# Deeper attention order, forget row as one fp32r product, squares taken from the accumulators, row norms with the factor last, and late weight splits moved, in a two-block fp32 kernel

## Chip, core and metric

The kernel runs on one core of a Trainium2 chip. The metric is the device time of one execution in microseconds. TensorE does the matmuls, VectorE (DVE), ScalarE (ACT) and GpSimd (POOL) the rest, SyncE (SP) issues most DMAs. The engines run side by side and meet at semaphores.

## What is computed

A sequence of 256 tokens of width 1024 passes a first stack of two layers and then one block of a second stack. Everything is fp32. Cut to what matters here:

```python
# layer 1 ("odd"): two kinds of attention side by side, then an output product
q, k, v, fl, cq, ckv, kr = split(x @ odd_w_in)
fcum = cumsum(log_sigmoid(fl + fgate_b))                 # 8 heads with a forget gate
s_fox = q @ k.T * 64 ** -0.5 + fcum[:, None] - fcum[None, :]   # causal, softmax, @ v
q2 = rms_norm(cq, q_norm_w) @ w_uq                       # 8 heads from latents, with rope
k2, v2 = rms_norm(ckv, kv_norm_w) @ w_ukv
x = layer_norm(alpha * x + concat(o_fox, o_mla) @ odd_w_out)
x = layer_norm(alpha * x + swiglu(x))                    # ffn0, ffn1: one per layer
# second stack, one block
h = x + mod2 * rmsnorm(short_gated_conv(modulate(rmsnorm(x, g0), mod0, mod1)), g1)
y = h + mod5 * rmsnorm(squared_relu_mlp(modulate(rmsnorm(h, g2), mod3, mod4)), g3)
```

The term of the query position in `s_fox` is the same for a whole softmax row, so the kernel adds only the key's, `neg_f`, of size 8 x 256 (one row for each head).

## The kernel before

**Weights.** All weights come in chunks (1 MB where nothing else is said), in one list in the order of their use. For each chunk SP loads `raw`, ACT copies it to `hi` in fp32r (L1130), DVE computes `lo` = raw - hi (L1559), and TensorE makes three fp32r products for every tile (hi with hi, hi with lo, lo with hi: L562 to L564 with the weights standing in the array, L569 to L571 with the activations there). There are six slots of such chunks, four in some stages. `split(upto)` in the ACT stream and in the DVE stream says how far the splitting has come; a call does all chunks up to the one named, in that engine's order, and ACT, DVE and TensorE each run their own program in order. So where a `split` stands decides what it delays. A TensorE product of a chunk waits for `lo_split`.

**Attention (profile 383 to 491 us).** `ODD_STEPS` is an order written by hand that all engines walk through: projections (`proj`), the norms of the two latents (`qn_sum`, `qn_out`, `kvn_sum`, `kvn_out`), the products from the latents (`uq`, `mla`), attention steps (`att`) and rows of the output product (`rows`). In step `att a` TensorE computes the scores of head a (L990 to L994), turns the probabilities of head a-1 (L1002) and multiplies those of head a-2 with the values (L1014, L1016). Heads 0 to 7 have the forget gate: each of the two score tiles (128 queries by 128 or 256 keys) is a plain fp32 product of `qz` and `kf` plus a second plain fp32 product that adds row a of `neg_f` to all queries (L991). DVE masks and finds the row maximum (L1964, L1968), ACT takes exponentials (L1417), DVE divides by the sum (L1973, L1975), TensorE turns, ACT copies the turned tile (L1432), TensorE multiplies, ACT and DVE split the outputs of each pair of heads (`o_hi`, `o_low`). `scores(a)` waits for the mask of head a-2. Heads 10, 11 and 12 have no other TensorE work between them.

**Latent norms.** ACT empties a projection bank into `cq` or `ckv` (L1368, L1370); at `qn_sum` and `kvn_sum` it squares those tiles (L1143), TensorE sums the squares with a column of ones (L676), ACT takes the root (L1149, with a change of the activation table before it, L1136), DVE the reciprocal (L1584), TensorE spreads it (L687), and DVE and ACT scale and split the latent (L1590, L1157, L1599).

**Row norms of the second stack.** `pre` and `preff` (the inputs of the convolution and of the MLP), `post` and `postff` (their outputs). Tokens lie in two halves h of 128, columns in two halves n of 512. `rms_std` on ACT squares all 1024 columns of a half with an accumulated sum (L1175) and takes the root (L1177). `modulated` on DVE waits for it, multiplies x with 1/rms and the scale row (L1680), then adds the shift row (L1685); `add_post` does the same from the accumulators (L1695, L1700). `turn` on TensorE (L660) turns the result, ACT and DVE split it (L1163, L1658), and the next products start. `ln_sum` and `ln_rest` are the layer norm ahead of `pre`. In this stretch DVE's `split(first["sc"] + 2)` and `split(first["mlp"] + 2)` stand before `modulated` of half 0.

**Other splits.** In the short convolution's third round (q = 3) `split(c + 3)`, `split(c + 4)` and `split(c + 5)` split the last three output chunks. In the MLP the first output chunk is split in round i = 3, after the turned hidden tiles (`mlp_hi`, `mlp_low`, L1515, L2080); in the last round the third-last output chunk is split after `mlp_hi(15)` and `mlp_low(15)`. Each TensorE round is a projection (`col`) and then rows of the output product.

The end of the chain is `postff`: square, root, reciprocal, two scalings, two additions for half 1, and four stores.

## Time and profile before

| | us |
|---|---|
| median of 3 runs | 1007.55 (1007.19 to 1009.74) |
| the profiled execution | 1008.01 |
| its span, first to last instruction | 1006.2 |
| TensorE busy | 962.0 |
| DVE busy | 644.7 |
| ACT busy | 461.5 |
| POOL busy | 59.4 |
| mean granted TensorE clock | 0.988 |

The span is 1.8 us shorter than the profiled execution's time, and that is 0.5 us above the median. "Busy" counts matmuls that lie in each other's pipeline once. A line of the timeline gives start, length, engine, line of the kernel, operation and tiles, how many records are merged (x16), and in brackets how long the engine was idle before it and what it waited for. Matmuls overlap in the pipeline: what one costs in a row of them is the distance from start to start, not its length. A plain fp32 product has two records. The granted clock is 1.00 at 2.4 GHz and 0.50 at 1.2 GHz.

### The profile page before, as it was taken

Reading aid. Unit: us, or ns where it says so; the run is one execution under the profiler, and the core shown is the slowest. Engines: PE = TensorE matmul, PEld = TensorE weight load, DVE = VectorE, ACT = ScalarE, POOL = GpSimd, SP = SyncE. Lnnn points to the kernel's source line nnn. Section 1 sums busy time; section 2 is a strip of 40 time slices with the busy share of each in tenths; the row PEclk is TensorE's granted clock in tenths of the full one; section 3 lists DMA queues with packets and bytes.
Section 4 is the critical chain, followed back from the end, with each engine's and each line's share of the span. In section 5 each row is a group of like instructions: output and inputs, shape, how many; then the busy total and the mean of one; then the engine's idle time right before and its main releaser. Section 6 shows DMA issues by size and latency. Waiting matters only on the chain.

```text
span 1006.2 us, 15135 instructions
## 1 busy us (share of the span) xinstructions
PE 962.0 (96%) x6561; PEld 876.1 (87%) x6561; DVE 644.7 (64%) x732; ACT 461.5 (46%) x553; POOL 59.4 (6%) x79
## 2 busy tenths in 40 slices
PE   6999989999999999999899999999899999999996
PEld 6999779999999899776699989997899888999884
DVE  5966895545455853565659778688677765455444
ACT  6456744443435355644454343445354434444342
POOL 2033000000000000120030000000000000000000
PEclk9999999999999999899999999999999999999999
DMA  8743466555564643212479999985455454565621
GB/s 259 242 131 126 159 196 218 180 184 193 175 202 128 188 147 111 84 43 85 153 279 329 387 310 343 306 320 194 172 179 179 145 183 163 176 201 170 204 87 42
DMA packets 122282, 190.52 MB, mean 189 GB/s; under 512 B 6566, under 2 KB 103080, under 8 KB 119144
## 3 DMA queue, kind: packets, MB, share of 16 engines
q1 hardware_dynamic: 115184, 156.94, 48.3%
q0 software_dynamic: 5616, 31.78, 8.6%
q8 instruction: 52, 0.85, 0.4%
q10 hardware_dynamic: 1416, 0.83, 0.3%
q14 instruction: 14, 0.11, 0.0%
HBM read 188.49 MB, written 1.05 MB: 188 GB/s over the span
## 4 chain that ended last, share of the span: by engine, by line
PE 79%; DVE 11%; ACT 6%; issue 2%; DMA 1%; DVEq 0%; ACTq 0%; POOL 0%
PE PS L562 15%; PE PS L564 15%; PE PS L563 15%; PE PS L569 9%; PE PS L570 9%; PE PS L571 9%; DVE lo L1559 4%; ACT hi L1130 2%; PE PS L695 1%; PE PS L660 1%; DMA raw<-even_w_in 1%; ACT hid L1417 1%; DVE r L1629 1%; PE PS L1014 1%; DMA sq<-norm_gains 1%
## 5 line engine op out<-in xcount | busy, mean ns | idle before, releaser
L1559 DVE TENSOR_TENSOR lo<-raw,hi 128x2048 fp32r<-128x2048 f32 (+2 forms) x150 | 336.0, 2259 | 163.8 <-ACT hi L1130 163.5
L562 PE MATMUL PS<-x_hi,hi 128*128 128x256 f32 x1320 | 376.1, 285 | 2.1 <-DVE x_lo L1756 2.1
L564 PE MATMUL PS<-x_hi,lo 128*128 128x256 f32 x1320 | 373.9, 283 | 0.0
L563 PE MATMUL PS<-x_lo,hi 128*128 128x256 f32 x1320 | 373.2, 283 | 0.0
L1130 ACT ACTIVATE hi<-raw 128x2048 fp32r<-128x2048 f32 (+2 forms) x150 | 277.8, 1879 | 8.5 <-DMA raw<-even_w_in 6.4
L562 PEld LDWEIGHTS PS<-x_hi,hi 128*128 128x128 f32 x1320 | 251.9, 191 | 4.5 <-DVE lo L1559 2.4
L563 PEld LDWEIGHTS PS<-x_lo,hi 128*128 128x128 f32 x1320 | 252.7, 191 | 1.7 <-issue 0.5
L564 PEld LDWEIGHTS PS<-x_hi,lo 128*128 128x128 f32 x1320 | 251.8, 191 | 0.0
L569 PE MATMUL PS<-hi,hid_hi 128*128 128x512 f32 x352 | 141.5, 402 | 6.0 <-DVE lo L1559 5.5
L570 PE MATMUL PS<-lo,hid_hi 128*128 128x512 f32 x352 | 139.8, 397 | 0.0
L571 PE MATMUL PS<-hi,hid_lo 128*128 128x512 f32 x352 | 139.1, 395 | 0.0
L569 PE MATMUL PS<-hi,x_hi 128*128 128x256 f32 (+1 forms) x256 | 82.8, 324 | 7.5 <-DVE x_lo L1658 3.4
L569 PEld LDWEIGHTS PS<-hi,hid_hi 128*128 128x128 f32 x352 | 66.6, 189 | 23.9 <-issue 9.5
L570 PE MATMUL PS<-lo,x_hi 128*128 128x256 f32 (+1 forms) x256 | 80.7, 315 | 0.0
L571 PE MATMUL PS<-hi,x_lo 128*128 128x256 f32 (+1 forms) x256 | 80.5, 315 | 0.0
L571 PEld LDWEIGHTS PS<-hi,hid_lo 128*128 128x128 f32 x352 | 66.5, 189 | 15.4
L570 PEld LDWEIGHTS PS<-lo,hid_hi 128*128 128x128 f32 x352 | 66.4, 189 | 15.1 <-issue 1.2
L569 PEld LDWEIGHTS PS<-hi,x_hi 128*128 128x128 f32 x256 | 49.8, 194 | 13.4 <-issue 8.1
L1215 ACT ACTIVATE gate_s<-PS 128x512 f32<-128x512 f32 x20 | 12.0, 598 | 104.0 <-PE PS L564 104.0
L571 PEld LDWEIGHTS PS<-hi,x_lo 128*128 128x128 f32 x256 | 49.7, 194 | 2.9
L570 PEld LDWEIGHTS PS<-lo,x_hi 128*128 128x128 f32 x256 | 49.7, 194 | 2.6
L1220 ACT ACTIVATE hid_hi<-hid 128x512 fp32r<-128x512 f32 x20 | 12.6, 632 | 81.6 <-DVE hid L1734 81.6
(276 smaller groups left out, 833.5 us busy)
## 6 DMA issues: line engine op xcount, KB each, us to landing
raw<-ffn_w_gate SPq DMA_DIRECT2D x22, 1024.0 KB, 5.4
raw<-ffn_w_up SPq DMA_DIRECT2D x22, 1024.0 KB, 5.4
raw<-ffn_w_down SPq DMA_DIRECT2D x22, 1024.0 KB, 5.0
raw<-mlp_w_in SPq DMA_DIRECT2D x16, 1024.0 KB, 5.6
raw<-mlp_w_out SPq DMA_DIRECT2D x16, 1024.0 KB, 5.0
sq<-ada_w POOLq DMA_DIRECT2D x12, 1024.0 KB, 6.2
r<-ada_w POOLq DMA_DIRECT2D x12, 1024.0 KB, 6.7
raw<-sc_w_in SPq DMA_DIRECT2D x12, 1024.0 KB, 5.3
```

The lines of the kernel that those rows point to most:

```text
L562: pe.matmul(dst, wh, hi, start=start, stop=False, skip_group_check=True)
L563: pe.matmul(dst, wh, lo, start=False, stop=False, skip_group_check=True)
L564: return pe.matmul(dst, wl, hi, start=False, stop=stop_, skip_group_check=True)
L569: pe.matmul(dst, hi, wh, start=start, stop=False, skip_group_check=True)
L570: pe.matmul(dst, hi, wl, start=False, stop=False, skip_group_check=True)
L571: return pe.matmul(dst, lo, wh, start=False, stop=stop_, skip_group_check=True)
L660: last = pe.transpose(PS[:, 2 * h + n, j * P:(j + 1) * P], src[:, h, o:o + P], ident)
L695: last = pe.matmul(PS[:, bank + n, :], ones[:, :], modrow[:, m, n * HB:(n + 1) * HB], start=True, stop=True)
L1130: act.activation(split_view("hi", c), split_view("raw", c), ACT.Copy).then_inc(hi_split, 1)
L1215: act.activation(gate_s[:, i % 2, :, :], bank2(6 - 2 * (i % 2)), ACT.Silu).then_inc(silu, 1)
L1220: act.activation(hid_hi[:, i % 3, :, :], hid[:, i % 2, :, :], ACT.Copy).then_inc(hi_done, 1)
L1559: dve.tensor_tensor(split_view("lo", c), split_view("raw", c), split_view("hi", c).bitcast(F32), ALU.subtract)\
```

## The change

- **Order of attention.** Step a turns head a-2 and multiplies head a-3; ACT copies the turned tile before the exponentials of head a; DVE masks head a, then divides head a-1. The pair outputs come one step later, and there is one more step, `att 18`.
- **Forget row.** `neg_both` holds the fp32r high part of `neg_f` in rows 0 to 7 and the rest in rows 32 to 39, for 128 and 256 keys side by side (384 columns); `pick` has ones in rows a and 32 + a of column a. One fp32r matmul per head opens both score tiles.
- **Squares of the latents.** ACT squares the projection bank right before it empties it; the kv squares get tiles of their own.
- **Row norms.** ACT squares each 512 columns as they come, turns the first sum into a bias with an Identity, and takes the root of the second plus that bias. DVE multiplies with the row first, and after the reciprocal does factor and add in one instruction per 512 columns. The unused square goes to PSUM (`rms_in`) or to `sq` (`rms_out`).
- **Splits.** `sc + 2` and `mlp + 2` on DVE go behind `turned_lo` of half 0; the convolution's last output chunks are split one place earlier; the MLP's first output chunk before the turned hidden tiles; its third-last one before the last `mlp_hi`/`mlp_low`.

```diff
@@ -98,13 +98,15 @@
         head_vec = sb("head_vec", [16, 4])
+        pick = sb("pick", [P, FOX_H], F32R)
...
         moments = sb("moments", [P, 2, 2])
-        sumsq = sb("sumsq", [P, 2])
+        sumsq = sb("sumsq", [P, 4])
+        part_sq = sb("part_sq", [P, 2])
@@ -156,6 +158,7 @@
             neg_f = sb("neg_f", [P, S], F32, odd)
+            neg_both = sb("neg_both", [P, 384], F32R, odd)
@@ -347,7 +350,7 @@
             ("mla", i) for i in range(5, 11)] + [("att", 8), ("rows", 0), ("att", 9), ("rows", 1), ("att", 10), ("att", 11),
-            ("att", 12), ("rows", 2), ("att", 13), ("att", 14), ("rows", 3), ("att", 15), ("att", 16), ("att", 17)]
+            ("att", 12), ("rows", 2), ("att", 13), ("att", 14), ("rows", 3), ("att", 15), ("att", 16), ("att", 17), ("att", 18)]
@@ -389,7 +392,7 @@
                     "op": ("ln0", "ln1", "ln2", "pre", "preff")}
-        EACH = {"r": 4, "st": 4, "mv": 2, "sq": 2, "std": 2, "t": 4, "x": 4, "turned": 4, "hi": 4, "lo": 4}
+        EACH = {"r": 4, "st": 4, "mv": 2, "sq": 6, "std": 2, "t": 4, "x": 4, "turned": 4, "hi": 4, "lo": 4}
@@ -666,7 +669,8 @@
                 else:
-                    parts = [([sq[:, 2 * q, :], sq[:, 2 * q + 1, :]], "sq", q + 1, 2) for q in range(t // 2)]
+                    o = 4 if name == "kvn" else 0
+                    parts = [([sq[:, o + 2 * q, :], sq[:, o + 2 * q + 1, :]], "sq", q + 1, 2) for q in range(t // 2)]
@@ -975,7 +979,7 @@
                 if a == 0:
-                    pe.wait_ge(sem("neg_f_ready"), 1)
+                    pe.wait_ge(sem("neg_f_ready"), 2)
@@ -983,12 +987,14 @@
                 b = a % 2
+                if a < FOX_H:
+                    pe.matmul(PS[:, b, 0:384], pick[:, a:a + 1].to_broadcast([P, P]), neg_both[:, :], start=True, stop=False,
+                              skip_group_check=True)
...
                     if a < FOX_H:
-                        pe.matmul(dst, qz[:, a, qs], kf[:, a // 2, 0:kw], start=True, stop=False)
-                        last = pe.matmul(dst, ident[:, a:a + 1].to_broadcast([P, P]), neg_f[:, 0:kw], start=False, stop=True)
+                        last = pe.matmul(dst, qz[:, a, qs], kf[:, a // 2, 0:kw], start=False, stop=True, skip_group_check=True)
@@ -1019,10 +1025,10 @@
                     scores(a)
-                if 1 <= a <= 16:
-                    turn_prob(a - 1)
-                if a >= 2:
-                    attend(a - 2)
+                if 2 <= a <= 17:
+                    turn_prob(a - 2)
+                if a >= 3:
+                    attend(a - 3)
@@ -1170,12 +1176,29 @@
-            def rms_std(name, h, src):
-                act.activation(r_tok[:, h, :], src, ACT.Square, accum_out=sumsq[:, h:h + 1]).then_inc(sig(name, "sq"), 1)
-                act.wait_ge(*sig_at(name, "sq", h + 1))
-                act.activation(std[:, h:h + 1], sumsq[:, h:h + 1], ACT.Sqrt, bias=eps_sb[:, 1:2], scale=1.0 / D)\
+            def rms_std(name, h, src, unused, ready):
+                for n in range(2):
+                    ready(n)
+                    act.activation(unused(n), src(n), ACT.Square, accum_out=sumsq[:, 2 * h + n:2 * h + n + 1])\
+                       .then_inc(sig(name, "sq"), 1)
+                    if n == 0:
+                        act.wait_ge(*sig_at(name, "sq", 3 * h + 1))
+                        act.activation(part_sq[:, h:h + 1], sumsq[:, 2 * h:2 * h + 1], ACT.Identity, bias=eps_sb[:, 1:2],
+                                       scale=1.0 / D).then_inc(sig(name, "sq"), 1)
+                act.wait_ge(*sig_at(name, "sq", 3 * h + 3))
+                act.activation(std[:, h:h + 1], sumsq[:, 2 * h + 1:2 * h + 2], ACT.Sqrt, bias=part_sq[:, h:h + 1], scale=1.0 / D)\
                    .then_inc(sig(name, "std"), 1)
+            def rms_in(name, before, h):
+                rms_std(name, h, lambda n: x_tok[:, h, n * HB:(n + 1) * HB], lambda n: PS[:, 2 * h + n, :],
+                        lambda n: act.wait_ge(*sig_at(before, "x", 2 * h + n + 1)))
+            def rms_out(name, which, h):
+                rms_std(name, h, lambda n: PS[:, 2 * h + n, :], lambda n: sq_all[:, n * HB:(n + 1) * HB],
+                        lambda n: wait_acc(act, which, h, n))
@@ -1365,25 +1388,22 @@
                 elif p <= 8:
+                    act.activation(sq[:, 2 * (p - 7):2 * (p - 7) + 2, :], bank, ACT.Square).then_inc(sem("norm_sq"), 1)
...
                 elif p == 9:
+                    act.activation(sq[:, 4:6, :], bank, ACT.Square).then_inc(sem("norm_sq"), 1)
...
             def qn_sum(_):
-                act.wait_ge(sem("odd_evac"), 9)
-                squares(cq, 4)
...
             def kvn_sum(_):
-                act.wait_ge(sem("odd_evac"), 10)
-                act.wait_ge(*norm("qn", "var", 1))
-                squares(ckv, 2)
@@ -1423,15 +1443,15 @@
             def attention(a):
+                if 2 <= a <= 17:
+                    act.wait_ge(sem("prob_turned"), a - 1)
+                    if a >= 4:
+                        act.wait_ge(sem("attended"), a - 3)
+                    act.activation(prob_t[:, a % 2, :], PS[:, 2, 0:384], ACT.Copy).then_inc(sem("prob_t_ready"), 1)
...
                     exps(a)
-                if 1 <= a <= 16:
-                    act.wait_ge(sem("prob_turned"), a)
-                    if a >= 3:
-                        act.wait_ge(sem("attended"), a - 2)
-                    act.activation(prob_t[:, (a - 1) % 2, :], PS[:, 2, 0:384], ACT.Copy).then_inc(sem("prob_t_ready"), 1)
-                if a >= 3 and a % 2:
-                    o_hi((a - 3) // 2)
+                if a >= 4 and a % 2 == 0:
+                    o_hi((a - 4) // 2)
@@ -1449,12 +1469,10 @@
             split(first["sc"] + 2)
-            act.wait_ge(*sig_at("ln3", "x", 2))
-            rms_std("pre", 0, x_tok[:, 0, :])
+            rms_in("pre", "ln3", 0)
...
             ln_std("ln3", 1)
-            act.wait_ge(*sig_at("ln3", "x", 4))
-            rms_std("pre", 1, x_tok[:, 1, :])
+            rms_in("pre", "ln3", 1)
@@ -1476,7 +1494,7 @@
                 c = at["sc", "c", q]
-                split(c + 3)
+                split(c + 3 + (q == 3))
@@ -1486,7 +1504,7 @@
                     sc_hi(0)
-                split(c + 4)
+                split(c + 4 + (q == 3))
@@ -1496,13 +1514,10 @@
             for h in range(2):
-                for n in range(2):
-                    wait_acc(act, "sc", h, n)
-                rms_std("post", h, PS[:, 2 * h:2 * h + 2, :].rearrange("p a n -> p (a n)"))
+                rms_out("post", "sc", h)
...
                     split(first["mlp"] + 2)
-                act.wait_ge(*sig_at("post", "x", 2 * h + 2))
-                rms_std("preff", h, x_tok[:, h, :])
+                rms_in("preff", "post", h)
@@ -1515,6 +1530,7 @@
+            split(c + 4)
@@ -1526,6 +1542,8 @@
                 act.activation(relu_s[:, i % 3, :, :], bank2(4 + i % 3), ACT.Relu).then_inc(sem("mlp_relu"), 1)
+                if i == NM - 1:
+                    split(c + 3)
@@ -1533,9 +1551,7 @@
             for h in range(2):
-                for n in range(2):
-                    wait_acc(act, "mlp", h, n)
-                rms_std("postff", h, PS[:, 2 * h:2 * h + 2, :].rearrange("p a n -> p (a n)"))
+                rms_out("postff", "mlp", h)
@@ -1672,33 +1688,33 @@
-            def modulated(name, h, shift, scale):
+            def modulated(name, before, h, shift, scale):
+                for n in range(2):
+                    dve.wait_ge(*sig_at(before, "x", 2 * h + n + 1))
+                    dve.tensor_tensor(half(r_tok, h, n), half(x_tok, h, n), modrow[:, scale, n * HB:(n + 1) * HB], ALU.mult)\
+                       .then_inc(sig(name, "t"), 1)
...
                 for n in range(2):
-                    dve.scalar_tensor_tensor(out=half(r_tok, h, n), in0=half(x_tok, h, n), scalar=rstd[:, h:h + 1],
-                                             in1=modrow[:, scale, n * HB:(n + 1) * HB], op0=ALU.mult, op1=ALU.mult)\
-                       .then_inc(sig(name, "t"), 1)
-                for n in range(2):
                     dve.wait_ge(*sig_at(name, "t", 2 * h + n + 1))
-                    dve.tensor_tensor(half(r_tok, h, n), half(r_tok, h, n), modrow[:, shift, n * HB:(n + 1) * HB], ALU.add)\
+                    dve.scalar_tensor_tensor(out=half(r_tok, h, n), in0=half(r_tok, h, n), scalar=rstd[:, h:h + 1],
+                                             in1=modrow[:, shift, n * HB:(n + 1) * HB], op0=ALU.mult, op1=ALU.add)\
...
                     wait_acc(dve, which, h, n)
+                    dve.wait_ge(*sig_at(name, "sq", 3 * h + 1 + 2 * n))
+                    dve.tensor_tensor(half(r_tok, h, n), PS[:, 2 * h + n, :], modrow[:, gate, n * HB:(n + 1) * HB], ALU.mult)\
+                       .then_inc(sig(name, "t"), 1)
...
                 for n in range(2):
-                    dve.scalar_tensor_tensor(out=half(r_tok, h, n), in0=PS[:, 2 * h + n, :], scalar=rstd[:, h:h + 1],
-                                             in1=modrow[:, gate, n * HB:(n + 1) * HB], op0=ALU.mult, op1=ALU.mult)\
-                       .then_inc(sig(name, "t"), 1)
-                for n in range(2):
                     dve.wait_ge(*sig_at(name, "t", 2 * h + n + 1))
-                    dve.tensor_tensor(half(x_tok, h, n), half(x_tok, h, n), half(r_tok, h, n), ALU.add)\
-                       .then_inc(sig(name, "x"), 1)
+                    dve.scalar_tensor_tensor(out=half(x_tok, h, n), in0=half(r_tok, h, n), scalar=rstd[:, h:h + 1],
+                                             in1=half(x_tok, h, n), op0=ALU.mult, op1=ALU.add).then_inc(sig(name, "x"), 1)
@@ -1905,7 +1921,8 @@
             base = first["odd"]
-            dve.memset(neg_f[:, :], 0.0)
+            dve.memset(neg_both[:, :].bitcast(F32), 0.0)
+            dve.tensor_tensor(pick[:, :], ident[:, 0:8], ident[:, 32:40], ALU.add)
@@ -1915,8 +1932,11 @@
                     link(dve.tensor_tensor(small[0:8, 3, :], small[0:8, 2, :], small[0:8, 1, :], ALU.add))
-                    dve.tensor_tensor_scan(neg_f[0:8, :], small[0:8, 3, :], small[0:8, 3, :], 0.0, ALU.add, ALU.bypass)\
-                       .then_inc(sem("neg_f_ready"), 1)
+                    link(dve.tensor_tensor_scan(neg_f[0:8, :], small[0:8, 3, :], small[0:8, 3, :], 0.0, ALU.add, ALU.bypass))
+                    for o, n in ((0, P), (P, S)):
+                        link(dve.tensor_copy(neg_both[0:8, o:o + n], neg_f[0:8, 0:n]))
+                        dve.tensor_tensor(neg_both[32:40, o:o + n], neg_f[0:8, 0:n], neg_both[0:8, o:o + n].bitcast(F32),
+                                          ALU.subtract).then_inc(sem("neg_f_ready"), 1)
@@ -1983,9 +2003,10 @@
                     masked(a)
-                    normalised(a)
-                if a >= 3 and a % 2:
-                    o_low((a - 3) // 2)
+                if 1 <= a <= 16:
+                    normalised(a - 1)
+                if a >= 4 and a % 2 == 0:
+                    o_low((a - 4) // 2)
@@ -2000,14 +2021,14 @@
             ln_rest("ln3", 0)
-            split(first["sc"] + 2)
-            modulated("pre", 0, 0, 1)
+            modulated("pre", "ln3", 0, 0, 1)
...
             turned_lo("pre", 0)
+            split(first["sc"] + 2)
...
             dve.memset(cv[:, :, :, 1 + S:2 + S], 0.0).then_inc(sem("cv_pad"), 1)
-            modulated("pre", 1, 0, 1)
+            modulated("pre", "ln3", 1, 0, 1)
@@ -2044,13 +2065,13 @@
                 i, c = q % 2, at["sc", "c", q]
-                split(c + 3)
+                split(c + 3 + (q == 3))
...
                 dve.wait_ge(sem("cv_ready"), q)
-                split(c + 4)
+                split(c + 4 + (q == 3))
@@ -2062,11 +2083,11 @@
             add_post("post", "sc", 0, 2)
+            modulated("preff", "post", 0, 3, 4)
+            turned_lo("preff", 0)
             split(first["mlp"] + 2)
-            modulated("preff", 0, 3, 4)
-            turned_lo("preff", 0)
             add_post("post", "sc", 1, 2)
-            modulated("preff", 1, 3, 4)
+            modulated("preff", "post", 1, 3, 4)
@@ -2080,6 +2101,7 @@
+            split(first["mlp"] + 4)
@@ -2089,6 +2111,8 @@
                    .then_inc(sem("mlp_hid"), 1)
+                if i == NM - 1:
+                    split(c + 3)
```

## Rows read from the trace of the kernel before

**Rows 1.** The page, busy time by engine (share of the span) and instructions.
```profile
PE 962.0 (96%) x6561; PEld 876.1 (87%) x6561; DVE 644.7 (64%) x732; ACT 461.5 (46%) x553; POOL 59.4 (6%) x79
```

**Rows 2.** Windows: length, busy PE, PEld, DVE, ACT, POOL, granted clock, DMA.
```profile
401.10:404.50 3.40, 3.40 (x13) 2.67 (x12) 0.64 (x4) 1.70 (x3) 0.00 (x0) 0.50 0.39 158
...
838.00:841.40 3.40, 3.40 (x10) 2.63 (x9) 1.61 (x2) 0.00 (x0) 0.00 (x0) 0.50 0.52 183
```

**Rows 3.** Timeline of TensorE, scores of head 0.
```profile
383.69 0.39 PE L991 MATMUL PS<-neg_f,const 128*128 128x128 f32 x2
383.91 0.60 PE L990 MATMUL PS<-kf,qz 128*128 128x256 f32 x2
```

**Rows 4.** Timeline of TensorE, head 8 and output rows of 512 columns.
```profile
454.24 0.82 PE L994 MATMUL PS<-km,qm 96*128 96x128 f32 x4
...
456.44 0.40 PE L570 MATMUL PS<-lo,x_hi 128*128 128x512 f32 x1
456.68 0.40 PE L571 MATMUL PS<-hi,x_lo 128*128 128x512 f32 x1
```

**Rows 5.** Timeline at the sums of the latent squares, ACT and TensorE.
```profile
398.60 1.14 ACT L1143 ACTIVATE sq<-cq 128x512 f32<-128x512 f32 x2
399.27 1.95 PE L676 MATMUL PS<-ones,sq 128*128 128x1 f32 x16 [1.20 <-ACT sq L1143]
...
401.54 1.28 ACT L1417 ACT_TABLE_LOAD   x1
...
419.58 1.02 PE L676 MATMUL PS<-ones,sq 128*128 128x1 f32 x8 [2.27 <-ACT sq L1143]
```

**Rows 6.** Waits of TensorE: total us, times, longest.
```profile
PE PS L1002 <- DVE hid L1975: 5.0, 4, 2.2
```

**Rows 7.** Timeline of the late heads and the drain, DVE and TensorE.
```profile
474.11 2.29 DVE L1559 TENSOR_TENSOR lo<-raw,hi 128x2048 fp32r<-128x2048 f32 x1 [1.43 <-ACT hi L1130]
...
479.02 0.55 PE L1002 MATMUL PS<-const,hid 128*128 128x128 f32 x3 [2.24 <-DVE hid L1975]
...
485.40 0.49 PE L1002 MATMUL PS<-const,hid 128*128 128x128 f32 x3
...
491.24 0.50 PE L569 MATMUL PS<-hi,x_hi 128*128 128x512 f32 x1 [0.93 <-DVE x_lo L1980]
```

**Rows 8.** Timeline of TensorE, its waits among the rope steps.
```profile
439.52 0.36 PE L952 MATMUL PS<-hid_hi,hi 128*96 128x256 f32 x1 [0.62 <-DVE kr L1946]
...
442.02 1.10 PE L943 MATMUL PS<-qm,const 96*96 96x256 f32 x4 [0.84 <-DVE qm L1956]
```

**Rows 9.** Timeline of DVE, scaling and splitting q's latent: first and last.
```profile
406.60 0.68 DVE L1590 TENSOR_TENSOR cq<-cq,PS 128x512 f32<-128x512 f32 x1
...
410.66 0.69 DVE L1599 TENSOR_TENSOR hid_lo<-r,hid_hi 128x512 fp32r<-128x512 f32 x1 [0.39 <-ACT hid_hi L1157]
```

**Rows 10.** Timeline before the short convolution, DVE and TensorE.
```profile
701.94 2.28 DVE L1559 TENSOR_TENSOR lo<-raw,hi 128x2048 fp32r<-128x2048 f32 x1
...
706.40 1.26 PE L660 MATMUL PS<-const,r 128*128 128x128 f32 x8 [2.89 <-DVE r L1685]
...
708.89 0.55 PE L569 MATMUL PS<-hi,x_hi 128*128 128x256 f32 x1 [1.23 <-DVE x_lo L1658]
```

**Rows 11.** Timeline of TensorE where it waited for a split of output weights.
```profile
794.97 0.47 PE L569 MATMUL PS<-hi,hid_hi 128*128 128x512 f32 x1 [0.78 <-DVE lo L1559]
...
836.95 0.47 PE L569 MATMUL PS<-hi,hid_hi 128*128 128x512 f32 x1 [2.13 <-DVE lo L1559]
...
985.07 0.47 PE L569 MATMUL PS<-hi,hid_hi 128*128 128x512 f32 x1 [2.21 <-DVE lo L1559]
```

**Rows 12.** Timeline of TensorE, the turn before the MLP.
```profile
806.87 1.26 PE L660 MATMUL PS<-const,r 128*128 128x128 f32 x8 [0.46 <-DVE r L1685]
```

**Rows 13.** Timeline of the closing norm, half 1, ACT and DVE.
```profile
999.32 1.02 ACT L1175 ACTIVATE r<-PS 128x1024 f32<-128x1024 f32 x1 [6.93 <-PE PS L571]
...
1002.42 1.28 DVE L1700 TENSOR_TENSOR x_tok<-x_tok,r 128x512 f32<-128x512 f32 x2
```

## The prediction

> **What bounds the kernel now.** I read the busy shares first, then TensorE's waits, then the granted clock, then the timeline at each gap. TensorE is busy for 96% of the span [rows 1]; DVE and ACT have room almost everywhere. So an edit gains only what it takes from TensorE's own work or from one of its few gaps, and work saved elsewhere is worth nothing. The gaps stand in five places, and the diff touches all of them: the attention stage (383 to 491 us), the norm before the short convolution (703 to 720), the norm between it and the MLP (795 to 820), the MLP's opening and end (837, 985), and the closing norm. Everything between them is an unbroken row of matmuls, which shifts as a block.
>
> A gap costs twice. After several gaps the granted clock is 0.50, that is 1.2 GHz and not 2.4, for a stretch of 3.4 us [rows 2]; five such stretches touch this diff (from 401.1, 421.6, 479.6, 708.3 and 838.0). Where TensorE has work for the whole stretch, it loses half of it, 1.7 us.
>
> **Attention stage: what goes.**
> - *Forget row.* Per head the two fp32 products with the forget row run over 128 and 256 columns. The 128-column one takes 0.22 us (383.69 to 383.91 [rows 3]), so both take 0.66. In their place stands one fp32r matmul of 384 columns. Fp32r matmuls of 512 columns follow each other at 0.24 us (456.44, 456.68 [rows 4]), so 384 take 0.18. That is 0.48 us for each of 8 heads: **3.8 us**, all on TensorE's path. The price is four small DVE instructions (copy, subtract, twice) behind the scan and three at the stage's start, well before the first head; DVE has idle time there.
> - *Squares at the accumulators.* ACT now squares the projection while it empties the bank, so at the sums TensorE no longer waits: 1.20 us at 399.27 and 2.27 us at 419.58 [rows 5], **3.5 us**. ACT's work is the same, only earlier; banks come free some 0.6 us later, but TensorE comes back to a bank after two more projections.
> - *Clock.* The stretches from 401.1 and 421.6 come right behind these two waits. With the waits gone I take both away: **3.4 us**.
> - *Deeper order.* TensorE waits 5.0 us in 4 places for the normalised probabilities [rows 6], and the third half-clock stretch follows the longest of them, 2.24 us at 479.02 [rows 7]: 1.7 us. Both are at stake: **6.7 us**. Two short waits for the rotary part (0.62 at 439.52, 0.84 at 442.02 [rows 8]) hang on DVE finishing the softmax of the same step; it no longer has to, which frees DVE about 1 us earlier: **1.4 us**.
>
> **Attention stage: what comes back.** The sum is 18.8 us, and TensorE, once ahead, meets the chains behind it.
> - Before `uq(0)`: from the first scaling to the last low half of q DVE and ACT need 4.75 us (406.60 to 411.35 [rows 9]), and both arrive late because two table loads (1.28 us each [rows 5]) and the exponentials of head 2 lie ahead. TensorE has only the kr projection and head 3 to cover it: a new wait of 1.4 us.
> - At the kv sum ACT still has the split of `w_ukv`, two evacuations, and a table load before and behind the root. TensorE waits for the reciprocal, for the probabilities of head 3 and, at head 2's output, for the bank that `o_low(0)` reads: some 2.2 us together.
> - Late heads: a split still sits in the DVE stream at head 12 (474.11 [rows 7]); the probabilities after it come 1.7 us too late even for the deeper order. Before head 8's output 0.6 us is added, since its bank waits for `o_low(3)`.
> - The drain: from the last scores (485.40) to the first output row (491.24) one head's whole chain takes 5.84 us [rows 7]. The deeper order leaves one more turn and output in it, which fills idle time, but the output of head 14 now also stands behind the chain of pairs: I take the drain as 6.6 us, and 1.4 us of the removed wait as not gained.
>
> Together 7.3 us come back, 11.5 net; a walk through the stage step by step gives 12.4. I take **12 us**. The ends: 18.8 if all new waits are covered, 6 if DVE and ACT are as late as they are now (then forget row and half the rest remain).
>
> **Norm before the short convolution.** Now: DVE splits a weight chunk (701.94, 2.2 us), then reciprocal, two scalings, two additions; TensorE's turn starts at 706.40 after 2.89 us, its first matmul at 708.89 [rows 10]. After: the product with the scale row needs no root and is done while ACT squares; the split goes behind; behind the root stand a reciprocal and one 0.7 us instruction. The root comes about when it does now (the two half squares need one more read and a small Identity, but the first starts 0.7 us earlier), just before the split ends at 704.2; so the first half comes at 704.5 and not 706.3, and the first matmul at 707.2: 1.7 us earlier. But the split now stands before the second half's `ln_rest`, which takes back 1.3; the second half comes only 0.7 to 0.9 us earlier and TensorE waits there instead. **0.9 us**, and the half clock from 708.3 changes nothing in it, since it only fills that wait.
>
> **Norm before the MLP.** The split of the last convolution weights moves ahead of the last convolution: the wait of 0.78 at 794.97 goes [rows 11]. The chain for half 0 (square, root, factor, add, square, root, factor, add, with a 2.2 us split inside) ends at 806.87 with a wait of 0.46 [rows 12]. With the split behind it and the factor last it is done by 803, while TensorE still has rows of half 1. The turn to first matmul time stays. 0.78 and 0.46 and what the second half gives: **1.4 us**.
>
> **MLP opening and end.** At 836.95 TensorE has waited 2.13 us for the split of the first output chunk, and a half-clock stretch follows from 838.0 [rows 2, 11]. The split now stands before the turned hidden tiles. Its data have been there for 20 us, ACT and DVE are idle in front of it, and `mlp_low(1)`, which it delays by about 1 us, is still done before TensorE is through the projection: 2.1 + 1.7 = **3.8 us**. At 985.07 the wait is 2.21 [rows 11]; the split moves ahead of `mlp_hi(15)` into idle time: **2.2 us**.
>
> **Closing norm.** Now after the last matmul: a square of 1024 (from 999.32), root, reciprocal, two scalings, two additions from 1002.42 to 1003.7 [rows 13]. After: half of the square and one product are done before; behind the last matmul remain a square of 512, the root, a product that now ends at about 1000.8, reciprocal, and two factor-and-add of 0.7: end at 1002.35. **1.4 us**.
>
> **A rule of the notes.** The new code puts an Identity between Square and the root. In this trace the exchange of tables costs 1.28 us each time [rows 5], and no row shows an Identity while the root's table is in. The Trainium skill, "ScalarE: Activation LUTs", in its section on table sets says that cheap functions such as identity are in every set, so no load would come. If it were otherwise, two loads in each of six norms would be a rival, priced below from the row.
>
> **Sum.** 12 + 0.9 + 1.4 + 3.8 + 2.2 + 1.4 = 21.7 us. The new waits (1.4, 2.2 and 1.7 us) are of the kind that brought the half clock before (2.24 us did): I take one new stretch, 1.7 us, so 20.0. The profiled execution took 1008.01 with a span of 1006.2; the median is 1007.55, 0.5 less. 1008.0 - 20.0 - 0.5 = **987.5 us**.
>
> **Rivals.**
> 1. *The clock keeps falling.* Three or more of the new gaps bring a half-clock stretch. For it: gaps of 1.2 to 2.3 us did so. Against: gaps of 2.21 us (985.07) and 0.9 to 1.6 us elsewhere did not. Two more stretches, 3.4 us: 991. The Trainium skill, "TensorE: Matmul & The Clock Gate", lets the clock fall only after a long idle gap; the trace shows it falling after 2.24 us, so the row decides.
> 2. *DVE and ACT bind in attention*, and the stage gives 6 and not 12: 993.5.
> 3. *All new waits are covered*: the stage gives 17 and no stretch is added, 6.7 us more than forecast: 981.
> 4. *Identity forces a reload*: 2 x 1.28 in each of six norms, of which about five are exposed: 12.8 us back, 1000.
> 5. *Slower: the heads become serial.* ACT's exponentials of head a now stand behind the copy of head a-2, and that behind TensorE's turn. If this closed into a ring with no overlap, each of 14 heads would take the 5.84 us of one chain [rows 7]. For heads 8 to 15 that is 47 us plus 8 for two splits, against 37 now (454.24 to 491.24 [rows 4, 7]), +18, with nothing left of the 12: 1008 - 9.7 + 18 = 1016. It decides only from 4.8 us a head on. Against it: the ring spans two steps, the scores of a+1 wait only for the mask of a-1, and the probabilities of a-2, which the turn needs, are finished while head a-1 is scored.
>
> **How the numbers follow.** The forecast (20 us, give or take 3) 0.58, rival 1 0.13, rival 2 0.13, rival 3 0.10, rival 4 0.03, rival 5 0.03. Range 981.5 to 994. A change under 0.3% (3 us) can't be told from none here. Faster by more 0.96, same 0.01, slower 0.03.
>
> **What would show it.** Forget row: one fp32r matmul of 384 columns per head, 0.18 us to the next. Squares: no wait before the sums, no half clock behind them. Order: TensorE's waits for probabilities under 2 us in all, and the first output row 12 us earlier. MLP: no wait at the first output chunk nor at the third-last one, no half clock. Closing norm: 1.3 us less between the last matmul and the end. The prediction is wrong if attention yields under 8 us, if table loads appear in the norms, or if gaps of over 2 us appear where there were none.

## The result and the profile after

Over 6 runs each, the kernel before takes 1007.94 us (1006.21 to 1009.74) and the changed one 980.84 us (979.70 to 983.36): ratio 0.973, interval 0.9711 to 0.975, or 25 to 29 us. The profiled execution of after took 980.15 us. The forecast was 987.5 us with a range from 981.5: the direction was right, the time came out 6.7 us shorter than forecast, and the range ended 0.7 us too high.

The page of after, busy time by engine, as [rows 1]:

```profile
PE 944.3 (97%) x6537; PEld 862.8 (88%) x6537; DVE 645.9 (66%) x737; ACT 466.6 (48%) x577; POOL 62.0 (6%) x79
```

TensorE's waits in after (line, releaser: total us, times, longest), as [rows 6]:

```profile
PE PS L572 <- DVE lo L1575: 3.9, 4, 1.9
PE PS L572 <- DVE x_lo L1674: 3.5, 3, 1.2
PE PS L663 <- DVE r L1701: 2.6, 2, 1.7
PE PS L1008 <- DVE hid L1995: 2.5, 3, 1.1
PE PS L565 <- issue: 1.3, 1, 1.3
```

The 5.0 us for probabilities have become 2.5 us in three places. Waits for latent squares are gone. L572's waits for `lo`, split weights, are what remains of 8.8 us before; their longest is 1.9 where it was 2.2, and the 1.9 stands in work that the change doesn't touch (127 us).

Windows over the stages of after (length, busy PE with its matmuls, granted clock, DMA share, GB/s), and, from before, its attention stage:

```profile
380.00:476.00 96.00, 87.35 (x569) 1.00 0.29 94
476.00:688.00 212.00, 209.68 (x1408) 1.00 0.87 306
688.00:708.00 20.00, 16.86 (x135) 1.00 0.44 143
708.00:787.00 79.00, 79.00 (x566) 1.00 0.57 184
787.00:812.00 25.00, 23.87 (x198) 1.00 0.55 194
```
```profile
383.00:491.00 108.00, 96.44 (x588) 0.95 0.25 84
```

In after the clock stands at its upper level, 2.4 GHz, through all of them; the five stretches that the prediction lists have no successor. One more, in work that the change doesn't touch, is in both profiles (134.8 us in before, 133.5 in after). TensorE's busy time in attention fell by 9.1 us (96.44 to 87.35): 3.8 of it is the forget row (as forecast), 5.1 the three stretches of 3.4 us in which matmuls ran at 1.2 GHz.

The timeline of after, TensorE in the attention stage: the forget row with the first product after it, the squares' sums, the new waits, and the first output row.

```profile
380.92 0.34 PE L991 MATMUL PS<-neg_both,pick 128*128 128x384 f32 x1
381.10 0.82 PE L997 MATMUL PS<-kf,qz 128*128 128x128 f32 x4
...
394.77 1.14 PE L680 MATMUL PS<-ones,sq 128*128 128x1 f32 x9
404.03 0.33 PE L565 MATMUL PS<-hid_hi,hi 128*96 128x256 f32 x1 [1.26 <-issue]
409.75 0.50 PE L680 MATMUL PS<-ones,sq 128*128 128x1 f32 x4
415.30 0.55 PE L1008 MATMUL PS<-const,hid 128*128 128x128 f32 x3 [0.99 <-DVE hid L1995]
416.49 0.62 PE L1020 MATMUL PS<-hid,v_tok 128*64 128x256 f32 x2 [0.64 <-DVE x_lo L2000]
428.58 0.36 PE L956 MATMUL PS<-hid_hi,hi 128*96 128x256 f32 x1 [0.60 <-DVE kr L1966]
431.08 1.10 PE L947 MATMUL PS<-qm,const 96*96 96x256 f32 x4 [0.86 <-DVE qm L1976]
465.12 0.55 PE L1008 MATMUL PS<-const,hid 128*128 128x128 f32 x3 [1.06 <-DVE hid L1995]
475.88 0.50 PE L572 MATMUL PS<-hi,x_hi 128*128 128x512 f32 x1 [0.93 <-DVE x_lo L2000]
```

The first output row comes at 475.88, 15.4 us earlier than [rows 7]; 2.5 of these were there before the first head, so the stage gave 12.8. Of the latent sums, both lines (394.77 and 409.75) stand without a wait. The norm before the convolution in after, TensorE:

```profile
688.19 1.32 PE L663 MATMUL PS<-const,r 128*128 128x128 f32 x8 [0.91 <-DVE r L1701]
690.74 0.36 PE L572 MATMUL PS<-hi,x_hi 128*128 128x256 f32 x1 [1.23 <-DVE x_lo L1674]
700.20 0.66 PE L663 MATMUL PS<-const,r 128*128 128x128 f32 x4 [1.72 <-DVE r L1701]
```

The turn waits 0.91 us where it waited 2.89 [rows 10], and half 1 waits 1.72 where it did not. The closing norm in after, ACT and DVE, as [rows 13]:

```profile
972.16 0.30 ACT L1187 ACTIVATE part_sq<-sumsq,eps_sb 128x1 f32<-128x1 f32 x1
972.23 0.69 DVE L1710 TENSOR_TENSOR r<-PS,modrow 128x512 f32<-128x512 f32 x1 [4.79 <-ACT sq L1183]
972.80 0.60 ACT L1183 ACTIVATE sq<-PS 128x512 f32<-128x512 f32 x1 [0.34 <-PE PS L574]
...
973.52 0.29 ACT L1190 ACTIVATE std<-sumsq,part_sq 128x1 f32<-128x1 f32 x1
...
974.39 1.42 DVE L1716 SCALAR_TENSOR_TENSOR x_tok<-r,rstd,x_tok 128x512 f32<-128x512 f32 x2
```

From the last matmul to the last instruction it takes 5.5 us, where before took 7.0. Between the Identity (L1187) and the root (L1190) no table is loaded, in this norm or any other (the last load of the kernel starts at 676.43 us); this is what the Trainium skill, "ScalarE: Activation LUTs", says in its section on table sets, and the trace agrees.

### The profile page after: what moved, and what is told of

The parts are those of the page before. It is cut to its first block, busy times and chain, and to the rows that moved or that the text cites. A ratio compares the mean times of both kernels' runs of the same rounds, so it can differ in the third digit from the quotient of the medians.

```text
span 978.3 us, 15123 instructions
## 1 busy us (share of the span) xinstructions
PE 944.3 (97%) x6537; PEld 862.8 (88%) x6537; DVE 645.9 (66%) x737; ACT 466.6 (48%) x577; POOL 62.0 (6%) x79
## 3 DMA queue, kind: packets, MB, share of 16 engines
HBM read 188.49 MB, written 1.05 MB: 194 GB/s over the span
## 4 chain that ended last, share of the span: by engine, by line
PE 80%; DVE 10%; ACT 5%; issue 3%; DMA 1%; DVEq 0%; POOL 0%; ACTq 0%
PE PS L565 15%; PE PS L567 15%; PE PS L566 15%; PE PS L572 10%; PE PS L574 9%; PE PS L573 9%; DVE lo L1575 3%; ACT hi L1136 2%; PE PS L699 1%; PE PS L663 1%; DMA raw<-even_w_in 1%; DVE r L1645 1%; ACT hid L1437 1%; DMA sq<-norm_gains 1%; ACT sq L1321 1%
## 5 line engine op out<-in xcount | busy, mean ns | idle before, releaser
L1136 ACT ACTIVATE hi<-raw 128x2048 fp32r<-128x2048 f32 (+2 forms) x150 | 278.1, 1880 | 10.2 <-DMA raw<-even_w_in 8.0
L572 PE MATMUL PS<-hi,hid_hi 128*128 128x512 f32 x352 | 141.2, 401 | 1.1 <-DVE lo L1575 0.7
L572 PE MATMUL PS<-hi,x_hi 128*128 128x256 f32 (+1 forms) x256 | 81.7, 319 | 7.7 <-DVE x_lo L1674 3.5
L572 PEld LDWEIGHTS PS<-hi,hid_hi 128*128 128x128 f32 x352 | 66.1, 188 | 17.5 <-issue 3.7
L572 PEld LDWEIGHTS PS<-hi,x_hi 128*128 128x128 f32 x256 | 48.8, 191 | 13.3 <-issue 8.1
```

What stands on the lines that cost most here:

```text
L572: pe.matmul(dst, hi, wh, start=start, stop=False, skip_group_check=True)
L1136: act.activation(split_view("hi", c), split_view("raw", c), ACT.Copy).then_inc(hi_split, 1)
```

## The experiments

Theory A: the terms are right, and what lies above them is the clock. Rival B: the surplus belongs to some part or to an effect outside the terms. First each part alone on the kernel before. All single parts carry the declarations of the change's new buffers, which turned out to matter. "Ratio" is always to before in the same job.

**Forget row alone.**

```
-last = pe.matmul(dst, ident[:, a:a+1]..., neg_f[:, 0:kw], start=False, stop=True)
+pe.matmul(PS[:, b, 0:384], pick[:, a:a+1]..., neg_both[:, :], start=True, stop=False)
```

> The kernel before with the forget row as one fp32r product and nothing else. The sum of the prediction: 8 heads at 0.48 us, 3.8 us less than before, ratio 0.996; the waits before the two sums of squares and the half-clock stretches behind them stay as they are. The rival, that the stage hangs on DVE and ACT and not on TensorE's work: under 1.5 us, the rest reappears as longer waits for the probabilities.

Measured 1001.68 us against 1007.40 in its job, -5.7 (ratio 0.994, 0.9917 to 0.9962), more than the term.

**Squares alone.**

```
+act.activation(sq[:, 2 * (p - 7):2 * (p - 7) + 2, :], bank, ACT.Square)
-squares(cq, 4)
-squares(ckv, 2)
```

> The kernel before with the latent squares taken from the accumulators and nothing else. Prediction's terms: 3.5 us of waits and two half-clock stretches of 1.7 us, 6.9 us, less a new wait of about 1 us before the products from q's latent: 5.5 to 7 us less, ratio 0.994. If the clock did not hang on these waits: 2.5 to 3.5 us, with the half clock still there.

Measured 999.88, -7.5 (0.9903 to 0.9953), over the upper end. In its profile both waits and both stretches are gone, as they should be if the clock hung on them; in return TensorE waits 6.6 us for probabilities, not 5.0.

**Order alone.**

```
-if 1 <= a <= 16: turn_prob(a - 1)
-if a >= 2: attend(a - 2)
+if 2 <= a <= 17: turn_prob(a - 2)
+if a >= 3: attend(a - 3)
```

> The kernel before with the deeper attention order and nothing else. If the parts add up: the waits for the probabilities in the late heads (5.0 us) shrink to under 2 and one half-clock stretch of 1.7 us goes, 3 to 5 us less, ratio 0.996. If the order only pays once the squares and the forget row have made TensorE faster: under 2 us.

Measured 996.39, -11.0 (0.9871 to 0.9918), over twice what was expected. The waits for the probabilities fell to 1.5 us, and the stretch in the late heads is gone.

**Splits alone.**

```
+            split(first["mlp"] + 4)
+                if i == NM - 1:
+                    split(c + 3)
...
-                split(c + 4)
+                split(c + 4 + (q == 3))
```

> The kernel before with only the three moved groups of splits (last convolution outputs, MLP opening, MLP end). Terms of the prediction: 0.8 + 3.8 + 2.2 = 6.8 us less, ratio 0.993; no wait at the first and at the third-last output chunk, no half clock in the opening. If the split only shifts the wait elsewhere: under 3 us.

Measured 995.65, -11.75 (0.9863 to 0.9906), 5 us over the terms; both waits are gone.

**Norms alone** (two half squares with an Identity, product with the scale row first, factor last, and `sc + 2` and `mlp + 2` on DVE behind `turned_lo`).

> Only the row norms' new order, on the kernel before. The forecast's terms 2.8 us (0.9, 0.5, 1.4). Theory A: 3 to 5 us, as the four microseconds that the whole change loses without them. Theory B (the norms' gain shows only behind the other parts): under 2.5 us.

Measured 1002.55 against 1008.78, -6.2 (0.9913 to 0.9958), above both theories.

Each single part gave more than its term, and together they make 42.2 us where the whole makes 27.1. Something may be counted in each of them. Next, the whole change less one part, always with all its buffers declared; the whole itself in that job:

> The whole change once more, as the yardstick of this job. Theory A (the half clock depends on the run: a gap of 1 to 2 us brings a half-clock stretch in some executions and not in others, and every 0.001 of mean granted clock is worth about 1.05 us): median 979 to 983, mean clock 0.994 to 0.999 over the runs, and the runs with the lower clock are the longer ones. Theory B (the change is worth more than its terms for a reason other than the clock): the same median, but time and clock don't go together.

Measured 981.4 (978.75 to 982.61), mean clock 0.995 to 0.997; the run with the lowest clock is the longest, as theory A has it, but five runs are few.

**Without the moved splits.**

> The change without its moved weight splits (last convolution weights, first and last output chunks of the MLP are split where they were). The waits before the first and the third-last output chunk come back (2.1 and 2.2 us), and some 0.8 in front of the norm before the MLP: 5.1 us of waits. Theory A: the clock part is by chance, so the mean clock falls by 0.002 to 0.003, 2 to 3 us more: 7 to 8 us over the whole change. Theory B (the parts only count once, the 11.8 us of the splits alone were partly others' gain): under 5 us. Theory C (each gap over 2 us always costs a stretch): 5.1 + 2 x 1.7 = 8.5 us and a half-clock stretch behind both gaps in the profile.

Measured 988.26, 6.9 over the whole change: B is out, and A's sum is just missed from below. Both waits are back in its profile, 2.14 us at 819.78 and 2.21 at 965.93, yet what stands behind them ran at full clock. Theory C is out: a gap of over 2 us doesn't always bring the half clock.

**Without the norms' new order.**

> The change without the row norms' new order. The forecast's terms: 0.9 before the convolution, some 0.5 in the norm before the MLP, 1.4 in the closing norm: 2.8 us over the whole change. Theory A: 3 to 4.5 us with the clock's part (the wait of 2.9 us at the turned halves is back). Theory B: the norms hold the gain that the forecast missed, over 6 us.

Measured 985.58, 4.2 over, as A has it.

**Without the order.**

> The change without the deeper attention order. The forecast: the 5.0 us of waits for normalised probabilities come back, less what the deeper order brought itself (about 3 us of new waits), so 2 to 3 us, and 1 to 3 us by the clock behind the 2.2 us wait. Theory A: 4 to 6 us over the whole change, mean clock 0.002 lower. Theory B (the order alone gave 11.0 us, all its own): 9 to 11 us.

Measured 990.20, 8.8 over. That is far more than A's 4 to 6 and just short of B's 9 to 11, but by A's mechanism: the mean clock is 0.990, 0.006 lower and not 0.002. TensorE's waits in this profile, its row for the probabilities, and the window behind the longest:

```profile
PE PS L1008 <- DVE hid L1995: 7.1, 5, 2.2
```
```profile
471.77 0.90 PE L1008 MATMUL PS<-const,hid 128*128 128x128 f32 x3 [2.24 <-DVE hid L1995]
```
```profile
471.00:477.80 6.80, 6.03 (x16) 4.24 (x17) 2.44 (x12) 1.94 (x7) 0.00 (x0) 0.51 0.00 0
```

Without the order, five waits make 7.1 us and not 2.5, and TensorE runs at 1.2 GHz for 6.8 us from within the wait of 2.24 on, where the kernel before had 3.4 us at this place. Another 3.4 us stand at 420.0, behind a wait of 2.13. In the attention stage of this profile TensorE waits 4.1 us longer than in after and loses 5.1 us to the clock, which makes the 9.3 us by which the stage is longer.

**Without the new squares.**

> The change with the latent squares taken behind the accumulators again. Two waits of 1.2 and 2.3 us come back: 3.5 us, less where a chain behind them (first low-rank product, kv sum) gives the time back. Theory A: 2 to 4 us of waits, plus 1 to 3 us by the clock, 0.001 to 0.003 lower: 4 to 6 us over the whole change. Theory B: 3.5 us or less with an unchanged clock.

Measured 985.54, 4.1 over the 981.4 of the job before (by the ratios to before, 0.9763 against 0.9721 and 0.9730, 3.3 to 4.2 us). TensorE in its profile, at the first sums, and the window behind:

```profile
397.11 2.98 PE L679 MATMUL PS<-ones,sq 128*128 128x1 f32 x16 [1.20 <-ACT sq L1148]
```
```profile
398.00:404.80 6.80, 6.80 (x31) 6.51 (x32) 2.89 (x12) 3.53 (x8) 0.00 (x0) 0.51 0.34 140
```

A wait of 1.20 us is back, and TensorE works at 1.2 GHz from 398.0 for 6.8 us; a second one, of 1.60 us at 416.88, has 3.4 us of half clock behind it. The stage is 5.5 us longer than in after, nearly all of it by the clock (10.2 us at half): its waits are only 0.7 us longer in all, since the two that are back cover others. By its time this run lies at A's lower end, by its profile it is A.

**Without the new forget row.**

> The change with the forget row's products in fp32 again, as before. The term: 8 heads x 0.48 us = 3.8 us of TensorE's own work. Theory A (terms right, surplus from the clock): 3.8 us over the whole change if TensorE sets the end at the first heads, a mean clock as with the whole change, or 2 us less if the time falls into waits that are there anyway (before the second low-rank product and at the kv sum). Theory B (the parts' surplus is in the attention stage): over 5.5 us.

Measured 981.78, 0.4 over (0.3 to 1.2 by the ratios), less than what A allowed at its low end. Against the trace of after, this one falls behind by 0.48 us a head for three heads; from 405 us on it falls no further behind. The five other heads stand beside waits: TensorE waits 1.5 us in 2 places for probabilities where after waits 2.5 us in 3. The whole stage is 1.4 us longer than in after.

**Late copy.** One wait on POOL, before the copy of the key's rotary part to all heads:

```
 pool.wait_ge(sem("kr_sum"), 1)
+pool.wait_ge(sem("qm_rot"), 1)
```

> The whole change, with one wait added on POOL: the copy of the key's rotary part to the 16 heads starts only when DVE has rotated the first pair of queries. The forecast had the wait of TensorE for these queries (0.84 us) vanish with the deeper order; it stayed, 0.86 us, and the DVE product in front of it takes 1.85 us where the same product takes 0.68 later, while POOL copies. Theory A (the two share something, POOL's copy slows the product): the product takes 0.7 us, the 0.86 us wait is gone, the copy still ends 8 us before the first scores that need it, and the kernel gains 0.9 us or less. Theory B (the product is slow for its own operands): it still takes 1.85 us and nothing is gained.

The product in after and in this kernel, on DVE, with POOL's copy:

```profile
428.59 1.89 POOL L538 COPY km<-kr 32x2048 f32<-32x2048 f32 x1 [1.65 <-DVE kr L1966]
429.17 1.85 DVE L1976 TENSOR_TENSOR qm<-sq,r 32x512 f32<-32x512 f32 x1
```
```profile
429.71 0.68 DVE L1977 TENSOR_TENSOR qm<-sq,r 32x512 f32<-32x512 f32 x1
430.54 1.88 POOL L539 COPY km<-kr 32x2048 f32<-32x2048 f32 x1 [3.06 <-DVE qm L1977]
430.62 1.03 PE L948 MATMUL PS<-qm,const 96*96 96x256 f32 x4
```

Theory A: the product takes 0.68 us, and the matmuls behind it have no wait. 979.03 us (978.20 to 980.11) against 981.4 and 980.84 in two other jobs, more than the 0.9 that A allowed; 1.1 us of it shows in the profile of this stage, the rest is within the spread of the runs. In after the product ends 0.54 us behind POOL's copy (430.48 to 431.02), as if it had stood still until then. The Trainium skill, "SBUF — State Buffer", in its section on who interferes with whom, describes a port pair that VectorE and GpSimd hold by turns, one blocking the other, also where a VectorE instruction has two inputs in SBUF and the GpSimd one reads SBUF, as here; these rows agree.

**Where nothing was edited.** Laid beside the norms-alone trace, the first one of before loses 0.6 us between 184 and 326, 0.3 between 356 and 365, 1.2 between 518 and 701 and 0.9 behind, in work that the part doesn't touch; beside the other traces the same. It loses them in rows of products that recur every 34 us, one chunk of the six in the ring. TensorE, the first and the 37th product of such a row (13th by this line, which has every third), in before:

```profile
182.38 0.28 PE L562 MATMUL PS<-x_hi,hi 128*128 128x256 f32 x1
...
186.69 0.29 PE L562 MATMUL PS<-x_hi,hi 128*128 128x256 f32 x1
```

In after, two products of the same row (15 further on in it):

```profile
182.52 0.28 PE L565 MATMUL PS<-x_hi,hi 128*128 128x256 f32 x1
...
186.72 0.28 PE L565 MATMUL PS<-x_hi,hi 128*128 128x256 f32 x1
```

36 products take 4.31 us in one, 4.20 in the other: 0.120 and 0.1167 us each. In after one chunk in six is quick; 176.07 to 180.38, just before, is 4.31 again. Slots 4 and 5 of the ring lie behind the small buffers. The change declares 32, 8 and 8 bytes more among these. Every buffer takes a multiple of 32 bytes in the built programs, and slots 4 and 5 start 64 bytes later.

> The kernel before, once more, profiled on the chip of this job. In the first trace of before, 24 products of 256 columns that read one of the wide weight slots take 2.88 us (0.120 us each) in stages that the change doesn't touch, where every other kernel of this case takes 2.80 us (0.1167 each). Theory A (placement: the new buffers are declared ahead of the two last weight slots and shift them by 64 bytes): this trace shows 0.120 us again. Theory B (that trace came from another chip or another day): it shows 0.1167 us here. For the clock: the half-clock stretches fall behind partly other gaps than in the first trace.

Its 36 products take 4.32 us again, so it is the kernel and not the chip. Time 1012.21 us. Half-clock stretches in its profile:

```profile
403.70:407.10 3.40, 3.40 (x12) 2.12 (x11) 1.46 (x8) 2.10 (x6) 0.00 (x0) 0.53 0.07 28
420.80:427.60 6.80, 6.80 (x26) 5.28 (x26) 2.21 (x10) 4.08 (x9) 2.48 (x2) 0.51 0.31 126
482.20:485.60 3.40, 3.40 (x10) 2.37 (x10) 1.23 (x6) 1.36 (x5) 0.00 (x0) 0.53 0.00 0
840.60:844.00 3.40, 3.40 (x10) 2.64 (x9) 1.76 (x2) 0.00 (x0) 0.00 (x0) 0.53 0.56 192
987.40:990.80 3.40, 2.98 (x7) 2.43 (x8) 2.47 (x2) 0.00 (x0) 0.00 (x0) 0.53 0.00 0
```

A sixth, from 711.1, fills a wait as in the first trace. Five of the six fall behind the same gaps as there, but the second is twice as long, 1.7 us more, and the last, at the third-last output chunk, is new: the same wait of 2.21 us had none behind it in the first trace. This goes a long way to explain the 7 us of spread of the kernel before: over its 13 runs in the job of the single parts, time and mean clock go together with correlation -0.85, about 1.05 us for each 0.001 (in the other jobs -0.72 to -0.88 and 0.7 to 1.05 us).

**Declarations alone.**

```
+        pick = sb("pick", [P, FOX_H], F32R)
-        sumsq = sb("sumsq", [P, 2])
+        sumsq = sb("sumsq", [P, 4])
+        part_sq = sb("part_sq", [P, 2])
```

> The kernel before with nothing but the change's new and widened buffers declared, none of them used. Theory A (placement): products that read weight slots 4 and 5 take 0.1167 us and not 0.120, about 2.6 us less over the kernel, and this is part of every single edit's gain above. Theory B: nothing moves, same time as before.

Measured 1003.83 us (12 runs) against 1007.58 (17 runs): -3.75 (0.9939 to 0.9972), for buffers that nothing uses. Its product rows from 182.27 take 4.20 us, like those of after. By the distances from start to start over its whole profile, the products of 256 columns take 3.0 us less than in before.

**Shifting one operand or the other.** First, 32 unused bytes between slots 0 to 3 and the activations:

```
+        sb("pad_x", [P, 8])
         x_tok = sb("x_tok", [P, 2, D])
```

> The version with the late copy, and an unused buffer of 32 bytes declared between weight slots 0 to 3 and the activations. The distance from the weights to the activations modulo 128 bytes is now for slots 0 to 3 what it was for slots 4 and 5 alone (96). Theory A1 (the distance of the two operands matters): all slots read at 0.1167 us a product and some 400 us of such products get 2.8% shorter: 8 to 12 us less than with the late copy alone, 967 to 971 us. Theory A2 (the address of the weights alone matters): slots 0 to 3 stay at 0.120 us, slots 4 and 5 go to an untried position; 977 to 982 us. Theory B (no placement): 979 us.

Measured 968.48 us (967.35 to 969.36), ratio to before 0.9597 (0.9566 to 0.9629). Second:

```
+        sb("pad_front", [P, 24])
         with ExitStack() as ring_raw:
...
+        sb("pad_wide", [P, 8])
         with ExitStack() as even:
```

> The version with the late copy, with 96 unused bytes in front of all buffers and 32 ahead of the wide area: every weight slot starts at 96 modulo 128 bytes, as only slots 4 and 5 did, but the distance to the activations is 0 for all slots. Theory A2 (the weights' own address matters): all slots at 0.1167 us, 967 to 971 us. Theory A1 (the distance matters): all slots at 0.120 us, also 4 and 5: 2 to 3 us more than with the late copy, 981 to 983 us. Theory B: 979 us.

Measured 984.03 us (982.54 to 984.39). TensorE in the first of these, two products 36 apart that were slow in after (176.07 to 180.38):

```profile
176.82 0.28 PE L567 MATMUL PS<-x_hi,hi 128*128 128x256 f32 x1
...
181.02 0.28 PE L567 MATMUL PS<-x_hi,hi 128*128 128x256 f32 x1
```

4.20 us; in the second all take 4.31 or 4.32, also those of slots 4 and 5. For these products the distance between the two operands decides (A1), not the weights' own address (A2): by the addresses in the built programs, the weights start 0 (slots 0 to 3) or 32 bytes (slots 4 and 5 of before) past the activations modulo 128 where it is slow, and 96 past them where it is quick. 64 was not tried.

The sizes take a second kind of product to fit. There are 3 x 1312 products of 256 columns; by the profiles they take 9.0 us less in the first kernel than with the late copy alone and 3.0 more in the second. But some 1050 products of 512 columns, with the hidden tiles standing and the weights moving, change as well. Here are nine of them in the first kernel and nine in the second:

```profile
831.64 0.39 PE L574 MATMUL PS<-hi,hid_hi 128*128 128x512 f32 x1
...
833.68 0.39 PE L574 MATMUL PS<-hi,hid_hi 128*128 128x512 f32 x1
```
```profile
843.54 0.39 PE L575 MATMUL PS<-hi,hid_hi 128*128 128x512 f32 x1
...
845.63 0.40 PE L575 MATMUL PS<-hi,hid_hi 128*128 128x512 f32 x1
```

That is 0.227 us each against 0.232. On average they take 0.2319 us with the late copy, 0.2276 in the first and 0.2332 in the second: 4.5 us less and 1.4 more. For them another distance is the quick one: the hidden tiles start 0 bytes past the weights modulo 128 in the first kernel, 96 in the second (slots 0 to 3 of before: 32, slow too). No run was made to test this rule by itself. So the second kernel's 5.0 us are 3.0 and 1.4 and some 0.5 at the start of the profile. In the first, 13.5 us of products went and 10.5 of time: 1.4 us went to a half-clock stretch at the start, the rest into longer waits. Why the distance matters no run here shows.

## Why the prediction was right and wrong

**The sum.** The single parts make 42.2 us, each with the declarations in it. Counting these once takes off 4 x 3.75: 27.2, against 27.1 measured. Each of the five has an interval of some 2 us to either side, so the fit is closer than it has a right to be, and it doesn't show that the parts add up: in the profiles the attention stage is 107.0 us long with the declarations alone, 3.5 shorter with the forget row, 4.3 with the squares and 6.6 with the order, 14.4 together, and 12.1 shorter in after. What holds is rival B, with the declarations as its cause. Against the 20.0 of the forecast:

- *A term was missing*: 3.75 us by the declarations. The sum of the prediction has no term for the first hunk of the diff, not even a bound. This is the step that failed most: with this term the forecast would have been 983.8, inside its range. No row of before could give the price; the declarations in the diff could have told that two weight slots move.
- *The half-clock stretch that was added* (1.7 us) did not come. After has new waits of 1.26, 0.99, 1.06 and 1.72 us, the kind that the forecast feared, and the windows stand at 1.00. With the four stretches removed and none added, 6.8 us of clock went in the profile, where the forecast had 5.1 net. That none came is in part luck: behind the same waits of 0.92 and 1.23 us before the convolution, late_copy has a stretch, from 689.9. Over the runs the lost clock (one minus the mean, times the time) fell from 13 to 4 us, an upper bound, since part of it lies in waits.
- *The rest*, 27.1 less 20.0, 3.75 and 1.7, is 1.7 us, in terms that were each a little small. The two profiles, laid side by side, say the same in another way. Of 27.9 us, 1.65 went at the start (below), 2.8 in the rows of products between the stages, and 23.7 in the six places that the forecast priced at 21.7: attention 12.8, convolution's norm 1.3, MLP's norm 1.8, its opening 3.9, its end 2.4, closing norm 1.5. (The sum is 28.1: a short new wait at 675.91, 0.2 us, goes the other way.)

**Attention** was 12, the profile shows 12.8, and made as it was foreseen: three stretches, 5.1 us of clock; waits from 11.8 to 8.6 us, 3.1 net (forecast 9.9 gone and 7.3 back); 3.8 of work. Its pieces, by step: the forget row's 0.18 us to the next product is exact at four heads (0.26 to 0.37 at the others). But the 3.8 us are not all gain: in company of the other parts it is worth 0.4 us by the times and 1.4 by the stage's length. The prediction put them as "all on TensorE's path", and this step was wrong: five of eight heads end in a wait of the chain behind. Alone it gave 5.7 less 3.75, 2.0 (3.5 by the stage's length). Squares: sums without a wait, as forecast; 3.8 alone and 4.1 in company against 3.5 plus 3.4 for the clock, so the clock's share came in full and the chain behind gave back waits: alone the stage lost 3.4 us of half clock and only 1.0 of its waits, and without the squares the stage of the whole change is longer by some 5 us of clock and 0.7 of waits. Order: 5.0 us of waits went to 2.5, where the prediction's own sign asked for under 2; worth 7.3 alone and 8.8 in company, where the sum had 6.7 + 1.4 less its part of the 7.3 that come back. The come-back was right in kind and place (1.26 before the q product against 1.4; 1.6 at the kv sum against 2.2; 1.06 at the late head against 1.7), and each a little too dear. The drain takes 5.95 us (469.93 to 475.88), not the 6.6 that were assumed; this is most of the 0.8 us.

**Rope waits.** Forecast: 1.4 us go, since DVE is freed earlier. They stayed at 0.60 and 0.86, against 0.62 and 0.84 [rows 8]. What holds them is not DVE's queue but POOL working beside it: late_copy shows it for the second. For the first I have only the row that DVE's normalisation took 1.45 us there beside POOL's product, which is argued and not shown.

**Norms.** Before the convolution 0.9 was forecast, 1.25 measured in the profile, with the new wait at half 1 as told. Closing norm 1.4 forecast, 1.5 measured (5.5 us behind the last matmul, not 7.0). Before the MLP 1.4 was forecast, with the split, and 1.8 measured. Without the norms' part the kernel loses 4.2 us where their terms made 2.8. In that profile a stretch of 6.8 us stands in and behind the wait of 2.9 us before the convolution (from 690.0), which the terms had at nothing; that this is the difference isn't shown.

**MLP opening and end.** 3.8 and 2.2 forecast, 3.9 and 2.4 measured; 6.9 us are lost without the moved splits, where the terms with the convolution's split made 6.8. This part was right, by reading wait and clock stretch off their rows. But the 1.7 us behind the wait is luck of the one execution: eight profiles have this wait, always 2.13 or 2.14 us, and the stretch stands behind it in three (both of before, norms_alone) and not in five (row, squares, order and declarations alone, no_splits). The wait of 2.21 us at the end, priced without a stretch, has one behind it in four of the same eight.

**The rivals.** 1 (clock keeps falling): the reverse came. Its case against, that gaps of 0.9 to 1.6 us elsewhere brought no half clock, misread the trace: there is a stretch at 134.8 behind a wait of 1.42 us. 2 (DVE and ACT bind): no. 3 (all new waits covered, 981) gave the time that came, for another reason: the waits are not covered. A right number would have hidden the missing term. 4: no reload at any Identity. 5: no ring; the gain has its sign.

The median is not the profiled execution: the first trace of before lost 1.7 us at its start, where the first products ran at half clock until 15.4 us and those of after did not. This 1.65 us is in the traces' difference and only by chance in the medians.

## What to carry over

Read a declaration as part of the change: it moves every buffer declared behind it, and here this was worth a seventh of the gain. Where equal matmuls are slow from one buffer and quick from another, compare the distances of their operands (which one is quick differs between kinds of products): 32 unused bytes gave 10.5 us here, against 11.75 for the best single edit with the declarations in it. And price work taken off the bound engine only after looking for the wait that its next chain will put there; leaving one part out of the finished kernel shows this (forget row: 1.4 us of the stage), the part alone on the old one does not (3.5).
